# Moving the first weight chunk up the load queue, and a small tap load to a second queue

## The reference

```
h = rms_norm(x, norm_mix_g)
proj = h @ w_in                                  # 1024 x 3840
a_val, a_gate, u, g_conv, g_ssm = split(proj)
y_conv = silu(layer_norm(conv31(a_val * sigmoid(a_gate)))) @ w_conv_out
y_ssm  = s5_branch(u)                            # linear recurrence, 16 groups of 64 states
x = x + (sigmoid(g_conv) * y_conv + sigmoid(g_ssm) * y_ssm) @ w_out
x = x + moe(rms_norm(x, norm_ffn_g))             # top 4 of 32 experts
out = rms_norm(x, norm_final_g)
```

## Time and profile before

| | |
|---|---|
| median of 3 runs | 1096.08 us (1095.37 to 1096.93) |
| profiled execution, own time | 1098.02 us |
| its span, first to last instruction | 1096.3 us |
| PE busy | 1056.0 us, 96% |
| DVE busy / ACT busy / POOL busy | 299.3 / 148.4 / 80.7 us |
| moved by the DMA queue of SP | 430.60 MB |
| mean granted clock of TensorE | 0.988 of full speed |

### The profile page before, as it was taken

How to read it: one execution, slowest core, us unless ns; L and a number is a source line. 1 busy time by engine, 2 the same in 40 slices (tenths; PEclk the granted TensorE clock), 3 DMA queues, 4 the chain that set the end, 5 groups by cost and what they waited for, 6 DMA issues and landing times.

```text
span 1096.3 us, 12167 instructions
## 1 busy us (share of the span) xinstructions
PE 1056.0 (96%) x4957; PEld 455.6 (42%) x4958; DVE 299.3 (27%) x686; ACT 148.4 (14%) x268; POOL 80.7 (7%) x155
## 2 busy tenths in 40 slices
PE   7999999999999999999999999999999999999996
PEld 6888876333333333333333333333323333333332
DVE  5999843311111111111111111111111011111122
ACT  3011403101010101111010000000000000000012
POOL 2986100000000000000000000000000000000000
PEclk9999999999999999999999999999999999999999
DMA  7947795899999999999999999999999999999995
GB/s 239 274 137 286 311 359 227 343 404 432 432 430 432 432 432 434 428 435 430 432 432 432 433 429 432 429 434 430 432 435 428 434 429 434 430 431 425 427 422 236
DMA packets 43223, 431.49 MB, mean 394 GB/s; under 512 B 6727, under 2 KB 22397, under 8 KB 25436
## 3 DMA queue, kind: packets, MB, share of 16 engines
q1 hardware_dynamic: 42924, 430.60, 94.1%
q10 hardware_dynamic: 272, 0.52, 0.1%
HBM read 430.06 MB, written 1.05 MB: 393 GB/s over the span
## 4 chain that ended last, share of the span: by engine, by line
PE 67%; DMA 30%; ACT 1%; DVE 1%; issue 0%; SPq 0%; another core or an unknown queue 0%; DVEq 0%
PE bank L1617 28%; DMA ring<-w_gate_up 27%; PE bank L1629 12%; PE bank L1362 10%; PE bank L1643 3%; PE bank L1555 3%; DMA ring<-w_down 3%; PE bank L1469 2%; PE bank L1497 2%; ACT area L759 1%; PE bank L1583 1%; PE bank L1608 1%; PE bank L1511 1%; PE bank L1457 1%; PE bank L1588 1%; DMA ring<-w_in 1%
## 5 line engine op out<-in xcount | busy, mean ns | idle before, releaser
L1617 PE MATMUL bank<-ring,area 128*64 128x512 f32 x2048 | 456.2, 602 | 16.5 <-DMA ring<-w_gate_up 16.5
L1617 PEld LDWEIGHTS bank<-ring,area 128*64 128x64 f32 x2048 | 150.7, 139 | 304.6 <-issue 271.1
L1629 PE MATMUL bank<-ring,area 128*64 128x512 f32 x1024 | 229.4, 599 | 6.4 <-ACT area L759 3.0
L1192 DVE TENSOR_SCALAR area<-bank 128x512 f32<-128x512 f32 x32 | 22.1, 692 | 669.9 <-PE bank L1617 669.9
L1629 PEld LDWEIGHTS bank<-ring,area 128*64 128x64 f32 x1024 | 71.8, 137 | 143.7 <-issue 133.6
L1362 PE MATMUL bank<-area,ring 128*128 128x256 f32 x480 | 107.8, 385 | 1.7 <-DMA ring<-w_in 1.7
L1362 PEld LDWEIGHTS bank<-area,ring 128*128 128x128 f32 x480 | 91.6, 192 | 16.1 <-DMA ring<-w_in 1.9
L765 ACT ACTIVATE area<-area 128x512 f32<-128x512 f32 x32 | 20.1, 629 | 483.7 <-DVE area L1192 483.7
L971 DVE SCALAR_TENSOR_TENSOR bank<-ring,spread,bank 128x256 f32<-128x256 f32 x174 | 71.5, 483 | 0.6
L1643 PE MATMUL bank<-area,spT 64*128 64x512 f32 x248 | 61.6, 615 | 0.7 <-ACT area L762 0.7
L1555 PE MATMUL bank<-rows,pick 128*64 128x512 f32 x256 | 62.2, 605 | 0.0
(11 more groups left out here) (263 smaller groups left out, 493.1 us busy)
## 6 DMA issues: line engine op xcount, KB each, us to landing
ring<-w_gate_up SPq DMA_DIRECT2D x51, 4096.0 KB, 45.0
ring<-w_down SPq DMA_DIRECT2D x25, 4096.0 KB, 43.9
ring<-w_gate_up SPq DMA_DIRECT2D x26, 1024.0 KB, 9.2
ring<-w_gate_up SPq DMA_DIRECT2D x13, 2048.0 KB, 41.6
ring<-w_down SPq DMA_DIRECT2D x18, 1024.0 KB, 12.7
ring<-w_in SPq DMA_DIRECT2D x15, 1024.0 KB, 8.2
ring<-w_down SPq DMA_DIRECT2D x5, 2048.0 KB, 13.4
ring<-w_conv_out SPq DMA_DIRECT2D x1, 3072.0 KB, 12.9
```

The lines of the kernel that those rows point to most:

```text
L1192: return v.tensor_scalar(gc, bank[4][:, :], 7.0, None, ALU.min)
L1617: last = mm(bank[4 + b][64 * h:64 * h + 64, :], heT[:, k % 4, k // 4 * 64:k // 4 * 64 + 64], fours(w, b, h), start=False, stop=(k == KD - 1))
L1629: last = mm(bank[b][64 * h:64 * h + 64, :], src[:, k % 4, k // 4 * 64:k // 4 * 64 + 64], w[:, k % 2, h * 512:h * 512 + 512], start=(k == 0 ...
```

## The change

Chunk 0 of w_in is issued right behind x, ahead of the ten parameter loads. `conv_w` leaves SP's queue: ACT issues it at the head of its own program, as two transfers of 16 and 15 rows, and PE waits for both.

```diff
             for t in range(TT):
                 sp.dma_start(x_sb[:, t, :], x[0, t * 128:t * 128 + 128, :]).then_inc(x_in[t], 16)
 
+            def load_win(c):
...
+            load_win(0)
             sp.dma_start(log_steps, ssm_log_step[0].rearrange("(t g) -> t g", g=2)).then_inc(par_in, 16)
...
-            load_win(0)
             load_win(1)
-            sp.dma_start(tap_rows, conv_w[0]).then_inc(tap_in, 16)
             for ri, src in enumerate((ssm_b_re, ssm_b_im)):
...
             s = nc.scalar
 
+            for r0, r1 in ((0, 16), (16, W)):
+                act.dma_start(tap_rows[r0:r1, :], conv_w[0, r0:r1, :]).then_inc(tap_in, 16)
             act.wait_ge(consts, 1)
...
             project(1, (0,))
-            pe.wait_ge(tap_in, 16)
+            pe.wait_ge(tap_in, 32)
             pe.wait_ge(params_sb, 1)
```

More of the change, by code:

```diff
@@ L355, in _ @@
                 sp.dma_start(x_sb[:, t, :], x[0, t * 128:t * 128 + 128, :]).then_inc(x_in[t], 16)
+            def load_win(c):
+                if c >= WRING:
+                    sp.wait_ge(win_pe, c - WRING + 1)
+                sp.dma_start(grid(at(c % WRING, CH), KD, 256),
+                             win_v[:, :, ORDER[c] * 256:ORDER[c] * 256 + 256]).then_inc(win_in[c % WRING], 16)
+            load_win(0)
             sp.dma_start(log_steps, ssm_log_step[0].rearrange("(t g) -> t g", g=2)).then_inc(par_in, 16)
```

## The result

The change made the kernel slower. Six runs of it have a median of 1102.25 us (1100.15 to 1103.73), six of the kernel before 1096.34 us (1095.37 to 1099.47): a ratio of 1.0053, with an interval of 1.0041 to 1.0066, or +5.9 us. The forecast was +0.86 us, 1096.9, with a range up to 1098.8. The profiled execution of the changed kernel took 1100.15 us (span 1098.4), the shortest of its six.

The account below looks back on a forecast made before the run. The prediction took PE to bound the kernel, its start shifting the end: chunk 0.7 us earlier, parameters 1.6 later, clock loss unchanged, so +0.86 on the median 1096.08 gives 1096.9 us; range 1094.6 to 1098.8.

Parts of the forecast that it names:

- What bounds the start: PE's first projection waits for w_in; without that wait 0.7 us earlier at most, h's slices being next.
- the parameters behind chunk 0: Ten small loads queue behind 1 MB on SP's queue, so PE's parameter rows (L1334) come 1.6 us later, at 9.4.
- the signal 1.1: From the last parameter packet to POOL's copy: 1.1 us, as read in the trace of before.
- The same spacing: From L1334 to h's slices all steps keep their distances: DVE begins at 11.0, PE's projection at 11.45, +0.86 us.
- The 1.76 us stay, in another place: PE's half clock in the projection's first 32 matmuls costs as much as before, 1.76 us, since PE still idles.
- rival 3: Clock stays low longer in the projection's first 32 to 48 matmuls: +2.6 us, 1098.7; chance 0.13.
- Rival 1: Clock holds through two short stops before the projection; DVE limits the end to -0.3 us, 1095.8; chance 0.14.
- One for one: A shift of PE at 20 us shifts the kernel's end by the same amount.
- ACT's issues: Two DMA issues at the head of ACT's program, taken as 0.7 us, cost nothing, as ACT idled 1.87 us.
- rival 4: conv_w's second transfer falls on one DMA engine, 1.85 us; sign: x lands after 5 us; +2.7, 1098.8; chance 0.04.
- Rival 2: Parameters not late at the start; projection at about 10.1, end moves by -1.7 us, 1094.4; chance 0.11.
- DVE as a limit: At the convolution's mean PE can gain 0.52 us before DVE must gain too; DVE could begin taps at 20.6.

Follow-up runs that it names:

- Chunk only: Kernel before with only chunk 0 of w_in moved behind x, ahead of the parameters; conv_w stays on SP: 1101.32 us, ratio 1.0056.
- taps only: Kernel before with only conv_w moved to ACT in 16 and 15 rows, chunk 0 still behind the parameters: 1095.4 us against 1095.84, ratio 0.9998.
- five and five: Kernel before with five parameter loads on SP, five on ACT, all before chunk 0; conv_w in two transfers behind chunk 1: 1093.82 us against 1095.32, ratio 0.9985.
- second trace of the kernel before: Another profiled execution of the unchanged kernel before, taken for comparison: own time 1095.37 us.
- second further trace: One of three later profiled executions of the changed kernel, with nothing altered, taken to see the clock's spread: own time 1101.63 us.

## Why the prediction was wrong, point by point

**What bounds the start.** Right in kind: without the chunk's wait, h would be last, and a new wait would take the place of the old. The projection was released by DVE's slices, and POOL's copy waited for the parameters, as the prediction named them.

**The step that failed is "the parameters behind chunk 0", by its size, and in it "the signal 1.1".** It put POOL's copy at 9.1; it came at 11.43. Of these 2.3 us some 0.9 are the end of chunk 0, at about 8.6 instead of 7.7: x was later by 0.8 in place of the 0.2 given it, and the rate was 352 GB/s, not 385. The other 1.4 lie between that end and the copy: 2.8 in place of 0.3 + 1.1. Chunk only shows that the second is the worse error: there x was on time and 50 of the small packets had gone by between 7.5 and 8.0 us, about where chunk 0 was expected to end, but the last 24 went only between 9.0 and 9.5, and the copy was at 11.26 all the same. The 1.1 had been read in the trace of before from the last packet to the copy. But there the issues had spread the loads out: most of their packets had gone by 5.0 us, and the last load's went up to 5.8. In the changed kernel all ten went within 0.7 us (8.5 to 9.2). Five more cost 0.92 us, and with nothing at all behind them the wait after the last packet was still some 2 us. Counted alike in both, from the end of the large transfer ahead of them to the copy, the ten loads took 6.99 - 4.75 = 2.2 us in the kernel before and 2.8 in the changed one. So the rows of before had 2.2 where the sum took 1.4; the other 0.6 is not explained.

By the Trainium skill, DMA: Bandwidth & Descriptors, section Queues, rings and completion order, a load's increment of its semaphore lands only after every earlier write of the same DMA engine, across its queues. Both the 0.18 us for each added load and the late copy of the parameters on ACT's queue (10.42) agree with it. That this rule is the cause was not isolated: no kernel here sent the small loads over different DMA engines.

**From the parameters to the projection.** "The same spacing" did not hold: PE's L1340 took 1.22 us in place of L1339's 0.71, since the clock was already low there (columns as in rows 5):

```profile
12.00:13.40 1.40, 1.33 (x5) 0.93 (x4) 0.00 (x0) 0.25 (x2) 1.01 (x6) 0.50 0.86 142
```

And PE followed the start of DVE's slices by 14.50 - 13.87 = 0.63 us, as in taps only and five and five, in place of the 0.45 reckoned with. With the hand-overs the projection followed the copy by 14.50 - 11.43 = 3.07 us, where 11.45 - 9.1 = 2.35 were reckoned with. With the 2.3 above this makes the 3.05 us by which 14.50 misses 11.45.

**The clock.** "The 1.76 us stay, in another place" was too low a guess in four of five traces: 1.5 to 3.05, as in rival 3, which had its place and its upper bound (1.76 more; 1.3 was seen) but only 0.13 of the chance. Rival 1 was not borne out by the change: its stop of 1.17 us before the projection was short, but 3.21 us of idle time stood ahead of L1335, and the clock fell there, at 11.9, before the projection had begun. Where the stop was 1.17 us with little other idle time ahead of it (taps only, five and five, one trace each) the clock stayed up.

**The sum** against the second trace of the kernel before, by the second further trace (1101.63): projection +3.85 (14.44 for 10.59), clock +1.29 (10.15 for 8.86), together +5.15 at the first expert (202.70 for 197.55), +6.26 in own time. The last 1.1 us come after the second expert; in the five traces that part is 0.2 to 1.1, and its source was not settled. "One for one" is right to that bound.

**What held.** ACT's issues cost nothing: 1.13 us for the two, and ACT was still idle for 1.48 us before x. The second transfer of `conv_w` was spread: its 15 rows went between 4.0 and 4.75 us, where the one engine of rival 4 would have taken 1.85. The sign named for it, x after 5 us, did appear (PE began on x at 5.05, and the second tile was there only at 6.67), but chunk only had the loss without it, so rival 4 falls. Rival 2's price, -1.7, is what five and five, another kernel, came near to with -1.5: the gain that the change was after was sized about rightly, and its condition, parameters that are not late, is the one that failed.

**DVE as a limit** was drawn too tight. With the first tap at 20.48, where the kernel before had 20.42, the taps-only kernel still asked for the convolution's mean (L1436) at 118.69, 1.0 earlier than the 119.70 of the earlier trace rows, and had the second expert at 222.89 in place of 223.91. In the kernel before DVE had waited for PE once more, among the taps, and that wait was gone:

```profile
27.09 0.42 DVE L953 TENSOR_TENSOR ring<-area,bank 128x256 f32<-128x256 f32 x1 [0.87 <-PE bank L1362]
```

The prediction did not count this row.

## What to carry to other kernels

A string of small loads can cost by its number, not its bytes: here five more of 4 KB cost 0.9 us, and ten of 27 KB in all took 2 us from their last packet to the copy with nothing behind them. So put them ahead of the first large transfer and issue them early from two engines, which gained 1.5 us here, rather than behind it. Read the time of a signal from the moment at which the queue is free for the loads to the instruction that waits, not from their last packet. And when a wait is removed, follow every load that the moved transfer now stands ahead of up to its consumer, since the last of ten decides.

## What the runs showed of the hardware that was not expected

Two transfers of together 95 KB on ACT's queue at the start put x off by 0.8 us, over three times what their bytes take at 400 GB/s (0.24), with a rate of 322 GB/s from 2.25 to 4.75 us.

Small loads on a second queue did not overtake a stream on the first: five us from the last issue to the copy, and 124 packets in 5.5 us.

The clock's loss at one and the same place differs by 1.6 us between executions of the same program, whose copies and starts of the projection agree within 0.15 us.

The four products that spread 1/rms took 0.71 us in the kernel before, at a granted clock of 1.00 (in the earlier trace rows the stretch from 8.0 us). In five and five they took 1.21, and the stretch around them (columns as in rows 5) reads

```profile
8.05:9.25 1.20, 1.20 (x5) 0.93 (x4) 0.00 (x0) 0.22 (x1) 0.83 (x5) 1.00 1.09 352
```

Its 1.00 is no reading: the first record of the clock in that trace is one of 1.00 at 9.11 us, and up to there the row prints 1.00 for want of a record. In the changed kernel the same products took 1.22 us at a recorded 0.50 (the stretch from 12.00 above). By that length, five and five ran them at the lower level. In the kernel before the first record of 1.00 is at 8.12, as they began; their length therefore hangs on when the clock comes up at the start, and that costs 0.5 us in the best version too. Why it came up a microsecond later there was not tried.
